# Two-path encoder step in fp32: the seven block products of the feed-forward layers with partial sums added on TensorE

## What is computed

```python
D_MODEL = 1024; D_FF = 2816
def rmsnorm(x, g):
    xf = x.astype(jnp.float32)
    y = xf * lax.rsqrt(jnp.mean(xf * xf, axis=-1, keepdims=True) + EPS) * g.astype(jnp.float32)
    return y.astype(x.dtype)
def swiglu_ffn(h, g, w_in, w_out):
    gate, up = jnp.split(rmsnorm(h, g) @ w_in, 2, axis=-1)
    return (jax.nn.silu(gate) * up) @ w_out
```

## Time and profile before

| | |
|---|---|
| three runs | 2632.05, 2634.39, 2635.95 us, median 2634.39 |
| profiled execution | 2632.12 us, span 2630.5 us |
| PE busy | 2469.0 us (94%), 17735 matmuls |
| DVE busy | 1797.3 us (68%) |
| ACT busy | 934.3 us (36%) |
| POOL busy | 358.6 us (14%) |
| HBM | 84 GB/s over the span |

### The profile page before, as it was taken

How to read it: one execution, slowest core, us unless ns; L and a number is a source line. 1 busy time by engine, 2 the same in 40 slices (tenths; PEclk the granted TensorE clock), 3 DMA queues, 4 the chain that set the end, 5 groups by cost and what they waited for, 6 DMA issues and landing times. The chain is left out here.

```text
span 2630.5 us, 44796 instructions
## 1 busy us (share of the span) xinstructions
PE 2469.0 (94%) x17735; PEld 2364.6 (90%) x17735; DVE 1797.3 (68%) x2930; ACT 934.3 (36%) x1680; POOL 358.6 (14%) x266
## 2 busy tenths in 40 slices
PE   6999999999999997999999979999999998999998
PEld 5899999989898976899999979999998787998998
DVE  7858587554545468858587277687777768868585
ACT  5424333121313233424342254334243544424242
POOL 0101013211111103101014211101022012101013
PEclk9999999999999998999999989999999998999998
DMA  4232323322323121322323432323223422322222
GB/s 115 80 92 84 89 74 90 90 77 65 92 65 92 57 64 57 88 81 80 97 77 88 130 99 72 96 81 88 76 85 106 118 78 65 88 81 85 85 83 66
DMA packets 394750, 222.12 MB, mean 84 GB/s; under 512 B 9105, under 2 KB 387057, under 8 KB 394577
## 3 DMA queue, kind: packets, MB, share of 16 engines
q1 hardware_dynamic: 389840, 205.22, 27.2%
q0 software_dynamic: 4544, 14.50, 1.7%
q10 hardware_dynamic: 192, 0.04, 0.0%
HBM read 206.01 MB, written 13.71 MB: 84 GB/s over the span
## 5 line engine op out<-in xcount | busy, mean ns | idle before, releaser
L681 DVE TENSOR_TENSOR wl<-raw,wh 128x1024 fp32r<-128x1024 f32 (+2 forms) x208 | 253.5, 1219 | 483.3 <-ACT wh L676 483.3
L1917 PE MATMUL ps<-xh,wl 128*128 128x288 f32 x1408 | 432.3, 307 | 96.1 <-DVE u L1258 44.1
L1917 PE MATMUL ps<-xl,wh 128*128 128x288 f32 x1408 | 418.4, 297 | 0.0
L1917 PE MATMUL ps<-xh,wh 128*128 128x288 f32 x1408 | 417.9, 297 | 0.0
L676 ACT CAST wh<-raw 128x1024 fp32r<-128x1024 f32 (+2 forms) x208 | 197.7, 950 | 581.4 <-PE ps L1861 581.4
L1917 PEld LDWEIGHTS ps<-xh,wl 128*128 128x128 f32 x1408 | 267.6, 190 | 125.0 <-DVE u L1258 50.1
L1763 POOL TENSOR_TENSOR gate<-gate,rstd 128x576 f32<-128x576 f32 x88 | 149.0, 1693 | 1374.7 <-DVE gate L1286 1374.7
L1917 PE MATMUL ps<-xmh,wl 128*128 128x288 f32 x1056 | 315.3, 299 | 0.9 <-DVE xml L1144 0.6
L1917 PE MATMUL ps<-xmh,wh 128*128 128x288 f32 x1056 | 315.5, 299 | 0.0
L1917 PE MATMUL ps<-xml,wh 128*128 128x288 f32 x1056 | 315.1, 298 | 0.0
L1861 PE MATMUL ps<-acth,wl 128*128 128x288 f32 x1408 | 304.2, 297 | 0.3
(11 more groups left out here) (283 smaller groups left out, 4608.5 us busy)
## 6 DMA issues: line engine op xcount, KB each, us to landing
raw<-in_ffn_w_in SPq DMA_DIRECT2D x176, 512.0 KB, 3.8
raw<-in_ffn_w_out SPq DMA_DIRECT2D x64, 512.0 KB, 3.9
raw<-in_ret_w_in SPq DMA_DIRECT2D x48, 512.0 KB, 3.9
raw<-in_ffn_w_out SPq DMA_DIRECT2D x32, 384.0 KB, 3.4
raw<-in_ret_w_out SPq DMA_DIRECT2D x32, 256.0 KB, 2.8
raw<-in_fox_w_kvf SPq DMA_DIRECT2D x16, 512.0 KB, 4.1
raw<-in_fox_w_q SPq DMA_DIRECT2D x8, 512.0 KB, 5.5
bias<-cum_scratch SPq DMA_DIRECT2D x16, 256.0 KB, 3.7
```

Source lines behind the costliest of these rows:

```text
L681: nc.vector.tensor_tensor(slot(wl, s, kt), raw[:, s, 0:kt, :], slot(wh, s, kt).bitcast(F32), ALU.subtract).then_inc(lo_ready, 1)
L1917: mm = nc.tensor.matmul(out, w, x, start=i < G12 and q == 0 and m == 0, stop=q == QUADS - 1 and m == 2, skip_group_check=i in (G12, S4, U22))
```

## The change

The same seven products; S3 is now called DIF. What changes:

- ScalarE copies G11's bank into S2's bank, and S2 is added onto it by TensorE; it copies that sum into S1's bank, and S1 is added onto it. It also copies the sums to SBUF (u2, u4) for the two additions that are left on VectorE (`late`: DIF + u4, `early`: U22 + u2). S4 lands on S1's bank and G12 on G11's; these two are the gate, and one VectorE instruction multiplies both by rstd, straight from PSUM (`gates`). GpSimd has no part in it any more.
- U22 and S4 of group g run within group g + 1 (`group`); those of a stage's last group stand alone behind it.
- The halves of k are tiles 0-3 and 4-7. x factors are made from h tile by tile (`x_first`, `x_mix`, `x_sums`, `x_second`): for a tile below 4 its first tokens and the difference of its token halves (`x_apart`, for S1), for a tile above three sums with its partner (for DIF, S2, U22) and the tile itself.
- The first group of an FFN makes G11 and S1, then DIF and S2, for each of four tiles (in the third FFN S2, G11, S1, DIF); VectorE adds its sums (`add_up`). rstd goes through columns of banks 5 and 7, and TensorE writes these banks once beforehand (`prime`), since they are later filled by ScalarE.
- The weights led in before a stage are those of five products; the weight sums of the second group are no longer made there.

```diff
-G11, S2, S1, S3, G12, S4, U22 = range(7)
+
+G11, DIF, S2, G12, S1, U22, S4 = range(7)
+FACTORS = 7
 ENTRY = [4, 5, 6, 0, 1, 2, 3]
 RING = 7
-BANK = [0, 1, 2, 3, 0, 2, 3]
-SUMS = [S1, S2, S3, S4]
-FACTORS, STEPS = 7, 5
+BANK = [0, 2, 1, 0, 3, 2, 3]
+SUMS = [S1, DIF, S2, S4]
...
 
-        def x_factor(n, hi, i, q):
+        def x_factor(hi, i, q):
 
             x, m = (xh, xmh) if hi else (xl, xml)
-            if i in (S1, S2, U22):
-                return m[:, q, (S1, S2, U22).index(i), :]
-            return x[:, 2 * q + (i in (G12, S4)), TA:T] if i in (S3, S4) else x[:, 2 * q + (i in (G12, S4)), 0:TA]
+            if i in (DIF, S2, U22):
+                return m[:, q, (DIF, S2, U22).index(i), :]
+            tile = x[:, q + (QUADS if i in (G12, S4) else 0), :]
+            return tile[:, TA:T] if i in (S1, S4) else tile[:, 0:TA]
...
+        LEAD = ((G11, DIF), (S2,), (G12, S1))
...
-                            factor_hi(act, a, G11)
-                            factor_hi(act, a, S2)
-                        if i == 0 and part == 0 and between is not None:
+                        alone, more = part == 0 and i == 0, i < n - 1
+                        if i:
+                            summed(g - 1)
+                            factor_hi(act, g, S1)
+                        act.wait_ge(made[G11], g + 1)
+                        def ahead(g):
+                            factor_hi(act, g, G11)
+                            factor_hi(act, g, DIF)
+                        before = part == 0 and i == 1
+                        if before:
+                            ahead(g + 1)
+                        if alone:
+                            nc.scalar.copy(p1, bank(g, G11)).then_inc(p1_ready, 1)
+                        else:
+                            if g >= 2:
+                                act.wait_ge(up_ready, g - 1)
+                            if part == 0 and i == 1:
+                                act.wait_ge(primed, FFNS.index(name) + 1)
+                                act.wait_ge(rstd_ready, rstds[name])
+                            nc.scalar.copy(bank(g, S2), bank(g, G11)).then_inc(seeded1, 1)
+                        if more and not before:
+                            ahead(g + 1)
+                        if alone and between is not None:
                             between()
...
+                        if i == 2 and part == 0 and entry is not None:
                             entry()
+                        if i >= 2:
+                            activated(g - 2)
+                        factor_hi(act, g, U22)
+                        if not alone:
+                            act.wait_ge(made[S2], g + 1)
+                            if g >= 2:
+                                act.wait_ge(gate_ready, g - 1)
+                            nc.scalar.copy(bank(g, S1), bank(g, S2)).then_inc(seeded2, 1)
+                            if g >= 2:
+                                act.wait_ge(up_ready, g - 1)
+                            nc.scalar.copy(u2[:, g % 2, :], bank(g, S2)).then_inc(u2_ready, 1)
+                        if more:
+                            factor_hi(act, g + 1, S2)
+                        factor_hi(act, g, S4)
                         if i:
...
+                            gated(g - 1)
+                        if more:
+                            factor_hi(act, g + 1, G12)
+                    summed(g0 + n - 1)
+                    activated(g0 + n - 2)
+                    split_hi(act, u1, u1 // 4, 0, n)
+                    gated(g0 + n - 1)
+                    activated(g0 + n - 1)
                     split_hi(act, u1 + 1, u1 // 4, 1, n)
...
+                    def late(g):
+                        dve.wait_ge(made[DIF], g + 1)
+                        dve.wait_ge(u4_ready, g + 1)
                         if g >= 2:
                             dve.wait_ge(act_ready, g - 1)
...
+                        nc.vector.tensor_tensor(up[:, g % 2, TA:T], bank(g, DIF), u4[:, g % 2, :], ALU.add) \
+                            .then_inc(late_ready, 1)
+                    def early(g):
+                        dve.wait_ge(made[U22], g + 1)
+                        if g > group0[name, 0]:
+                            dve.wait_ge(u2_ready, g - FFNS.index(name))
+                        nc.vector.tensor_tensor(up[:, g % 2, 0:TA], bank(g, U22), u2[:, g % 2, :], ALU.add) \
+                            .then_inc(up_ready, 1)
+                    def gates(g):
+                        dve.wait_ge(made[G12], g + 1)
+                        dve.wait_ge(made[S4], g + 1)
                         if g >= 2:
                             dve.wait_ge(prod_ready, g - 1)
...
+                        b = 4 * (g % 2)
+                        nc.vector.tensor_tensor(gate[:, g % 2, :].rearrange("p (a t) -> p a t", a=2), ps[:, b:b + 4:3, 0:TA],
+                                                rstd[:, :].rearrange("p (a t) -> p a t", a=2), ALU.mult).then_inc(gate_ready, 1)
+                    def gated(g):
+                        dve.wait_ge(silu_ready, g + 1)
+                        dve.wait_ge(up_ready, g + 1)
+                        nc.vector.tensor_tensor(up[:, g % 2, :], up[:, g % 2, :], gate[:, g % 2, :], ALU.mult) \
+                            .then_inc(prod_ready, 1)
+                    def activated(g):
+                        dve.wait_ge(act_hi, g + 1)
+                        nc.vector.tensor_tensor(actl[:, g - g0, :], up[:, g % 2, :], acth[:, g - g0, :].bitcast(F32),
+                                                ALU.subtract).then_inc(act_ready, 1)
+                    def add_up(g, k):
+                        dve.wait_ge(p1_ready, k + 1)
+                        dve.wait_ge(made[S2], g + 1)
+                        if g >= 2:
+                            dve.wait_ge(up_ready, g - 1)
+                        nc.vector.tensor_tensor(u2[:, g % 2, :], bank(g, S2), p1, ALU.add).then_inc(added, 1)
+                        dve.wait_ge(made[S1], g + 1)
+                        dve.wait_ge(added, 2 * k + 1)
+                        nc.vector.tensor_tensor(bank(g, S1), bank(g, S1), u2[:, g % 2, :], ALU.add).then_inc(added, 1)
...
+                        g = g0 + i
+                        alone, more = part == 0 and i == 0, i < n - 1
+                        if alone:
+                            add_up(g, FFNS.index(name))
+                        if i:
+                            late(g - 1)
+                            factor_lo(dve, g, S1)
+                        if more:
+                            weight_sums(dve, g + 1, (S1, DIF))
+                            factor_lo(dve, g + 1, G11)
+                            weight_sums(dve, g + 1, (S2,))
+                            factor_lo(dve, g + 1, DIF)
+                        if i == 2 and part == 0 and entry is not None:
+                            entry()
+                        if i >= 2:
+                            activated(g - 2)
+                        if alone and roots is not None:
+                            roots()
+                        if part == 0 and i == 1 and roots is not None:
+                            take_rstd_apart(FFNS.index(name))
+                        if i:
+                            early(g - 1)
+                        factor_lo(dve, g, U22)
+                        if more:
+                            factor_lo(dve, g + 1, S2)
+                        if i:
+                            gates(g - 1)
+                        factor_lo(dve, g, S4)
+                        if more:
+                            weight_sums(dve, g + 1, (S4,))
+                        if i:
+                            gated(g - 1)
+                        if more:
+                            factor_lo(dve, g + 1, G12)
+                    late(g0 + n - 1)
+                    activated(g0 + n - 2)
+                    split_lo(dve, u1, None, 0, n)
+                    early(g0 + n - 1)
+                    gates(g0 + n - 1)
+                    gated(g0 + n - 1)
+                    activated(g0 + n - 1)
...
+            def block_product(n, g, b, i):
+                pe.wait_ge(factor_ready[i], g + 1)
+                later = not (isinstance(g, int) and g < 2)
+                if i == G11 and later:
+                    pe.wait_ge(gate_ready, g - 1)
+                if i == DIF and later:
+                    pe.wait_ge(up_ready, g - 1)
+                if i == S2:
+                    pe.wait_ge(seeded1, g - n)
+                if i == S1:
+                    pe.wait_ge(seeded2, g - n)
+                if i in (U22, S4):
+                    pe.wait_ge(late_ready, g + 1)
+                for q in range(QUADS):
+                    factor_block(b, i, q)
+            def group(n, g, b, second=None):
+                for i, before in ((G11, 0), (DIF, 0), (U22, 1), (S2, 0), (S4, 1), (G12, 0), (S1, 0)):
+                    block_product(n, g - before, 1 - b if before else b, i)
```

(35 more changed lines are left out.)

589 lines of the change are left out of this document (289 added, 300 removed).

## The result

| | before | changed |
|---|---|---|
| median | 2633.63 us (4 runs, 2632.05 to 2635.95) | 2573.69 us (4 runs, 2572.20 to 2577.18) |
| profiled execution | 2632.12 us, span 2630.5 | 2572.65 us, span 2571.0 |

A forecast was written before the change was run, and what follows sets the result against it. TensorE, busy 94% of the span, was taken as the bound, with its waits. Stages -84.0, ends +12.6, thin unit +1 and openings -3.3 sum to -73.7 us from 2632.1; with 2.3 for the median, 2561 us, range 2545 to 2588.

The forecast's parts named there:

- Stages, -84.0: Steady groups of the twelve stages: every queue fits, TensorE waits for nothing, so 84.0 us go.
- their ends, +12.6: At each of twelve stage ends TensorE waits 1.05 us for the u4 copy and late sum: +12.6 us.
- Rival 1: Steady loop: one 0.5 us wait remains per group as VectorE slips, +38 us, 2599 us in all; chance 0.09.
- Rival 4: Steady loop held by VectorE's amount of work alone, other waits come: same time, 2634 us; chance 0.03.
- The thin second output unit, +1: After a stage's last S4, the second output unit has 4.55 against 4.8 us: +1 us, 0 to 6.
- The unknown prices: ScalarE's seed copy into PSUM taken at 0.39 us, up to 0.69; gates reading two banks 0.75, up to 0.9.
- Rival 3: ScalarE's seed copies, if slow into PSUM, block TensorE twice a group: 2667 us at 3.8 us copies; chance 0.03.
- The openings, -3.3: Starts of the four feed-forward layers: +4.3, -3.1, -11.6 and +7.1 us, together -3.3, each good to 5 us.
- The rule on VectorE and GpSimd: Second opening: whole-instruction lockout beside GpSimd's squares could cost 13.6 us instead of 8, the sum 5.6 us worse.
- Rival 2: Openings: GpSimd's squares hold VectorE up fully (+11), late products run at half clock (+9): 2581 us; chance 0.10.
- Why TensorE waited before the change: In-group results (p1 for G12, u2 for S4) come from queued engines; VectorE, at its limit, loses 1.1 us beside GpSimd.

The follow-up runs named there:

- Experiment 4: Changed kernel with S1 before G12 in the last group of each of the twelve stages: 2560.96 us, ratio 0.9722.
- experiment 7: Changed kernel without GpSimd's sums of squares of h, except one square, before the second and fourth feed-forward layers: 2563.24 us, ratio 0.9739.
- experiment 5: Kernel before without GpSimd's multiplication of the gate by rstd (left out, so output is wrong): 2541.53 us, ratio 0.9656.
- experiment 6: Changed kernel with one 576-wide GpSimd multiplication, into an unused buffer, put back into each group: 2575.26 us, ratio 0.9784.
- experiment 12: Kernel before, gate multiplied by rstd on VectorE, ScalarE casting S1's weights before acth, VectorE's actl between low parts of S1 and S3: 2541.78 us, ratio 0.9664.
- experiment 9: Changed kernel with S1 before G12 in each stage's last group, and G11 before S1 in the second feed-forward layer's first group: 2559.52 us, ratio 0.9729.
- experiment 1: Changed kernel with U22 and S4 moved back to the end of their own group: 2864.47 us, ratio 1.088.

## Why the prediction was right in size, and where not

- **Stages, -84.0, and their ends, +12.6.** Right: 70.8 us gained where -71.4 stood. Experiment 4 took the ends away alone: their waits were the 1.05 us each that was summed up from rows, but an end cost 1.37. Both terms were some 3 to 4 us too small, since 0.1333 us a matmul is a little too much (87.3 and 16.5 by experiment 4), and that they cancel is luck. Rivals 1 and 4 fell with it: no wait is left in the steady loop.
- **The thin second output unit, +1.** It cost nothing: 51.20 us in both kernels.
- **The unknown prices.** The copy from bank to bank took 0.383 us, 0.39 was taken; the 576-wide multiplication from PSUM 0.75. Rival 3 fell: even at five copies the kernel is 38 us faster than before.
- **The openings, -3.3.** This is the step that failed: they cost 11.2. The first came 2.7 us later than laid out, the third 3.1, the fourth 1.2 sooner, and the second 9.9 later (-3.1 forecast, +6.8 measured). Its parts, by the trace of the changed kernel: tile 0 is taken at 958.17, 556.2 us after the end of the first layer's last stage; I had laid it as in the kernel before, 554.7 (967.42 - 412.75). From there the last xml ends at 1009.86, 5.1 us behind the layout: GpSimd's squares cost 10.2 us, of which 8 had been charged, and the tiles with their weight work were 2.9 us longer than laid out without any GpSimd. From that xml to the end of the products TensorE took 3.4 us instead of 2. Behind them 24.0 us pass to the third group where I counted 22.2, with a granted clock of 0.86 on average. Together 9.8. The 1.5 us ahead of tile 0 are not the change's. In the same work of the retention the clock was granted at 0.72 in one execution and at 1.00 in the other (changed kernel, then the kernel before; bounds, length, PE busy, clock, DMA share, GB/s), and over all kernels here, of the old code and the new, tile 0 comes 552.8 to 556.6 us after that stage:

```profile
451.97:457.97 6.00, 5.78 (x34) 0.72 0.73 203
...
462.75:468.75 6.00, 5.79 (x45) 1.00 0.66 206
```

- **The rule on VectorE and GpSimd.** VectorE lost 10.2 us beside the squares (seven additions and four multiplications, not eight additions as I counted), between my 8 and the 13.6 that I worked out from whole instructions. The first estimate was 2.2 us too low and the second 3.4 too high. The Trainium skill, "SBUF — State Buffer", section "SBUF: two separate sides", says that of such a pair the one that comes second is held up until the other's instruction is over. The trace agrees: the multiplication at 974.89 took 1.28 us instead of 0.52 and ended 0.31 us after GpSimd's step (experiment 7). What that comes to over a stretch the rule alone does not give.
- **Rival 2** (2581) came nearer than its chance of 0.10 said: the openings cost 14.5 us more than forecast, where it had 20.
- **Why TensorE waited before the change.** The place was right (G12 for p1, S4 for an addition of its own group, though that is u5, line 1258, and not u2 as I wrote), the cause half right. I named VectorE's limit and its 1.1 us beside GpSimd, and the order of the products. What I passed over stands in the earlier trace rows: Silu's 388.8 us of idle before it, released by GpSimd, 4.4 us in each of 88 groups, on the engine that makes p1 and U22's cast behind it. ScalarE is busy 36%, and I followed only its copy p1, not what held the copy up. The length of that idle time is not the loss: in experiment 5, where next to nothing is lost, 172.2 us of it are left. Rival 4 leaned on VectorE's amount of work; of the 8.14 us that part 1 lost, the runs put 5.6 down to one slow step at the head of ScalarE's queue and 2.4 to the load on VectorE. Experiment 5 shows that the order of the products need not be touched; experiment 6, that the new order bears GpSimd's load on VectorE, which the old one did not.

So the change is a real cure: it takes the waits out of the steady loop, 84 us, and gives 13 back at the stage ends and 11 in the openings, which the small cure (experiment 12) does not. What remains open: what made the first and third opening later than laid out, by 2.7 and 3.1 us here and by 4.5 to 6.7 in the executions of experiments 4, 7 and 9, and why they differ so between executions. No run was made for these.

## What to carry to other kernels

An engine that is busy a third of the time can hold up the one that is busy 94%: look at what its idle time waits for, and then at what is queued behind that wait. Before an order of products is turned over, take the suspected step out by itself; one such run showed here that the whole loss in the stages went with one instruction, and the edit that follows from it is some 30 us better. A layout that defers work makes the steady loop safe and pays at every start and end, so count how many there are.

## What was not expected of the hardware

- ScalarE copies 128x288 from one PSUM bank to another in 0.383 us, against 0.393 from PSUM to SBUF.
- A sum on VectorE with two SBUF inputs (0.69 us alone) took 1.80 us beside a GpSimd multiplication of two different tensors (1.74 us), and 1.52 beside one of a tensor by itself (1.44 to 1.46 us). In these cases VectorE's instruction took 0.06 to 0.08 us more than GpSimd's step.
- With one wait of 2.5 us per group (experiment 1) the clock of a stage was granted at 0.91 on average, where the changed kernel has 1.00 with no such waits, and the kernel before 1.00 with shorter ones (0.8 us at most for u); part 1 lost 28.0 us, of which the waits are 18.1.
